# One streaming-encoder layer on one core: 1/rms by a diagonal, another load order, two splits and two bank plans moved

## What is computed

```python
h = rmsnorm(x, g_pre_mix)                   # x * rsqrt(mean(x*x) + eps) * g, a token per row
z = h @ w_in                                # 1024 -> 1440 mixer columns + 2048 gate logits
q = rmsnorm(z[:, 0:384], g_q) @ w_uq        # latent attention: queries
ckv = rmsnorm(z[:, 384:640], g_kv)          # latent keys and values
a = latent_attention(q, ckv, rope(kpe))     # prompt (chunk-causal) and sample against the cache
b = window_attention(rope(qs), rope(ks), vs, sinks)   # chunks of 64 frames, 192 keys, a sink per head
m = sigmoid(gate_a) * (a @ w_branch[0]) + sigmoid(gate_b) * (b @ w_branch[1])
x = x + rmsnorm(m @ w_out, g_post_mix)
x = x + rmsnorm(swiglu(rmsnorm(x, g_pre_ffn)), g_post_ffn)
```

## Time and profile before

| | us |
|---|---|
| median of three runs | 919.78 |
| lowest, highest | 918.79, 921.39 |
| the profiled execution itself | 920.1 |
| its span, first to last instruction | 918.3 |
| TensorE busy in it | 880.5 |
| VectorE busy | 485.5 |
| ScalarE busy | 390.5 |
| GpSimd busy | 75.8 |
| mean granted clock of TensorE | 0.997 |

### The profile page before, as it was taken

How to read it: one execution, slowest core, us unless ns; L and a number is a source line. 1 busy time by engine, 2 the same in 40 slices (tenths; PEclk the granted TensorE clock), 3 DMA queues, 4 the chain that set the end, 5 groups by cost and what they waited for, 6 DMA issues and landing times.

```text
span 918.3 us, 13750 instructions
## 1 busy us (share of the span) xinstructions
PE 880.5 (96%) x5457; PEld 799.9 (87%) x5457; DVE 485.5 (53%) x745; ACT 390.5 (43%) x771; POOL 75.8 (8%) x73
## 2 busy tenths in 40 slices
PE   4999999999999988999999899999999999999997
PEld 3888899989977776998878899999999998888885
DVE  5523522433344555564668877777777774343124
ACT  5311422244454556452565544445545443332112
POOL 0300198050030000000000000000000000000000
PEclk9999999999999999999999999999999999999999
DMA  6523246062240000654623232223333226322202
GB/s 266 162 87 79 73 112 202 8 188 83 76 106 1 1 1 2 184 176 180 217 92 92 69 90 74 78 82 92 93 92 92 76 86 223 98 69 92 70 24 115
DMA packets 101452, 91.92 MB, mean 100 GB/s; under 512 B 8480, under 2 KB 85296, under 8 KB 101248
## 3 DMA queue, kind: packets, MB, share of 16 engines
q1 hardware_dynamic: 95072, 85.93, 30.3%
q10 hardware_dynamic: 5424, 3.25, 1.2%
q0 software_dynamic: 896, 1.92, 0.6%
HBM read 79.60 MB, written 12.40 MB: 100 GB/s over the span
## 4 chain that ended last, share of the span: by engine, by line
PE 91%; ACT 3%; DVE 3%; DMA 1%; issue 1%; DVEq 0%; ACTq 0%
PE ps L1142 27%; PE ps L1144 26%; PE ps L1143 26%; PE ps L1316 2%; PE ps L1365 1%; PE ps L1327 1%; PE ps L1412 1%; PE ps L1286 1%; PE ps L1359 1%; PE ps L1290 1%; DVE nm_c L1687 1%; ACT probs L871 1%; PE ps L1389 1%; PE ps L1399 1%; DMA x_t<-in_x_prompt 1%
## 5 line engine op out<-in xcount | busy, mean ns | idle before, releaser
L1624 DVE TENSOR_TENSOR wlo<-raw,whi 128x1024 fp32r<-128x1024 f32 x59 | 77.4, 1315 | 212.1 <-ACT whi L800 204.6
L800 ACT ACTIVATE whi<-raw 128x1024 fp32r<-128x1024 f32 x59 | 62.0, 1056 | 178.6 <-PE ps L1144 169.6
L1142 PE MATMUL ps<-h_hi,wlo 128*128 128x320 f32 x288 | 90.9, 316 | 1.9 <-DVE z L1664 1.0
L1144 PE MATMUL ps<-h_hi,whi 128*128 128x320 f32 x288 | 89.0, 309 | 0.0
L1143 PE MATMUL ps<-h_lo,whi 128*128 128x320 f32 x288 | 88.9, 309 | 0.0
L1142 PE MATMUL ps<-sc_hi,t_lo 128*128 128x320 f32 x252 | 78.0, 309 | 3.9 <-ACT u L1057 2.9
L1144 PE MATMUL ps<-sc_hi,t_hi 128*128 128x320 f32 x252 | 77.8, 309 | 0.0
L1143 PE MATMUL ps<-sc_lo,t_hi 128*128 128x320 f32 x252 | 77.8, 309 | 0.0
L1047 ACT ACTIVATE t_hi<-wd 128x512 fp32r<-128x512 f32 x84 | 52.8, 629 | 58.6 <-DVE wd L1883 52.8
L1142 PE MATMUL ps<-whi,gu_lo 128*128 128x512 f32 x190 | 74.0, 390 | 0.3 <-DVE gu_lo L1955 0.3
L1143 PE MATMUL ps<-wlo,gu_hi 128*128 128x512 f32 x190 | 73.9, 389 | 0.0
(11 more groups left out here) (302 smaller groups left out, 2135.4 us busy)
## 6 DMA issues: line engine op xcount, KB each, us to landing
raw<-in_w_gate_up SPq DMA_DIRECT2D x44, 512.0 KB, 3.8
raw<-in_w_down SPq DMA_DIRECT2D x22, 512.0 KB, 3.7
raw<-in_w_in SPq DMA_DIRECT2D x16, 512.0 KB, 4.0
raw<-in_w_in SPq DMA_DIRECT2D x12, 480.0 KB, 4.3
gates_scratch<-gate_s SPq DMA_DIRECT2D x16, 320.0 KB, 2.4
gate_r<-gates_scratch SPq DMA_DIRECT2D x8, 640.0 KB, 4.0
raw<-in_w_branch SPq DMA_DIRECT2D x8, 512.0 KB, 4.7
raw<-in_w_out SPq DMA_DIRECT2D x8, 512.0 KB, 5.6
```

Source lines behind the costliest of these rows:

```text
L800: act.activation(whi[:, r % 2, :] if to is None else to, raw[:, r, :], ACT.Copy).then_inc(w_hi, 1)
L1142: pe.matmul(out, left[1], right[0], start=first, stop=False, skip_group_check=not own_group)
L1144: return pe.matmul(out, left[0], right[0], start=False, stop=last, skip_group_check=not own_group)
L1624: dve.tensor_tensor(lo[:, place, :], raw[:, r, :], hi[:, place, :].bitcast(F32), ALU.subtract).then_inc(w_lo, 1)
```

## The change

1. **1/rms apart from the norm weight.** VectorE multiplies x by the norm weight into a new tile `xg` as soon as both have landed (`h_gain`). 1/rms goes on the diagonal of a 128x128 tile `diag_r` (two of them in turn), and `h_turn` multiplies each block of `xg` by it with an ordinary fp32 matmul in place of a transpose.
2. **Loads.** `gpre_b` moves from ScalarE's queue to SyncE's, second in order; slot 0 then comes ahead of tile 1, and slot 1 ahead of tile 2.
3. **Order in the opening.** A `Sqrt` on a constant stands ahead of the first statistics on ScalarE. TensorE does 24 transposes of the identity into bank 7 before the first turn. On TensorE the turn of tile 1 moves between the two slots of tile 0's product; on ScalarE and VectorE the statistics of tile 1 and the split of slot 1 move behind tile 0's parts.
4. **z chunks in rotating banks**: chunk c and tile t in bank (5c + t) mod 8, and gate 0 waits for 10, gate 1 for 12 emptied banks. TensorE's, and VectorE's, loops there are written out.
5. **Late splits.** On ScalarE and VectorE what belongs to the eighth gate slot (the logits' copy and the split of slot 21) moves behind the 15 transposes' jobs.
6. **Sinks.** `job_bank` is turned by one, so the last two jobs lie in banks 6 and 7. VectorE writes the sinks when all but these two are emptied, and does its last job behind them. TensorE waits for the last two jobs only before the first two `chunk_values`, which use banks 6 and 7.

```diff
 def job_bank(j):
-    return 4 + j % 4 if j < JOBS1 else (j - JOBS1) % 4
+    return 4 + (j + 3) % 4 if j < JOBS1 else (j - JOBS1) % 4
...
             load_x(0)
-            load_x(1)
+            sp.dma_start(gpre_b[:], g_pre_mix.to_broadcast([P, D])).then_inc(gpre_in, 16)
             for j in range(2):
                 load(j, win_v[:, 2 * j:2 * j + 2, 0:IN_CHUNK], IN_CHUNK)
-            for t in range(2, TILES):
+                load_x(j + 1)
+            for t in range(3, TILES):
                 load_x(t)
...
         def _(act):
-            act.dma_start(gpre_b[:], g_pre_mix.to_broadcast([P, D])).then_inc(gpre_in, 16)
...
             act.wait_ge(eps_rdy, 1)
+            act.activation(sd_h[:, 7:8], eps_c[:, 0:1], ACT.Sqrt).then_inc(table_rdy, 1)
...
-            for j in range(8):
+            def first_logits(j):
                 if j >= 2:
-
                     act.wait_ge(g_st[j % 2], 16 * (j // 2))
                 logits_out(G0, 0, j, gate_s, 2 * (j % 2))
-            for j in range(JOBS1):
+
+            for j in range(7):
+                first_logits(j)
+            for j in range(3 * TILES):
+                job(j)
+            first_logits(7)
+            for j in range(3 * TILES, JOBS1):
                 job(j)
...
             def h_turn(t):
-                pe.wait_ge(h_norm, t + 1)
+                pe.wait_ge(h_xg, t + 1)
+                pe.wait_ge(h_diag, t + 1)
...
-                        ins = pe.transpose(ps[:, 5 + n % 3, k * P:(k + 1) * P], x_t[:, t, c:c + P], ident[:])
+                        ins = pe.matmul(ps[:, 5 + n % 3, k * P:(k + 1) * P], xg[:, t, c:c + P], diag_r[:, t % 2, :],
+                                        start=True, stop=True)
...
             pe.wait_ge(const_rdy, 1)
+            for n in range(24):
+                pe.transpose(ps[:, 7, 0:P], ident[:], ident[:])
             h_turn(0)
             for t in range(TILES):
-                if t + 1 < TILES:
+                if t and t + 1 < TILES:
                     h_turn(t + 1)
...
+                    if t == 0 and k == 2:
+                        h_turn(1)
...
-            with pe.Fori(0, 2) as it:
+            for chunk in (1, 2):
+                def z_bank_free(t):
+                    if 5 * chunk + t >= 8:
+                        pe.wait_ge(bank_empty, 5 * chunk + t - 7)
+
                 for j in range(4):
-                    tall(it * 4 + (4 + j + 1), j % 2, IN_CHUNK, h_hi, h_lo, 2 * j, KD - 1,
-                         lambda t: pe.wait_ge(bank_empty, it * 5 + (t + 1)), z_mm)
-
+                    tall(4 * chunk + j + 1, j % 2, IN_CHUNK, h_hi, h_lo, 2 * j, KD - 1, z_bank_free, z_mm, 5 * chunk)
+
+            for j in range(8):
+                pe.wait_ge(w_lo, G0 + j + 1)
+                if j < 2:
+                    pe.wait_ge(bank_empty, 10 + 2 * j)
+                b = 2 * (j % 2)
+                wide(j % 2, h_hi, h_lo, (b, b + 1), 0, KD, KD).then_inc(w_used, 1)
             pe.wait_ge(bank_empty, 15)
...
-            job_emptied(pe, JOBS1 - 2)
-            job_emptied(pe, JOBS1 - 1)
...
+                if c < 2:
+                    job_emptied(pe, JOBS1 - 2 + c)
...
+            def h_gain(t):
+                dve.wait_ge(x_in[t], 16)
+                dve.tensor_tensor(xg[:, t, :], x_t[:, t, :], gpre_b[:], ALU.mult).then_inc(h_xg, 1)
+
...
-                dve.scalar_tensor_tensor(out=x_t[:, t, :], in0=x_t[:, t, :], scalar=r_h[:, t:t + 1], in1=gpre_b[:],
-                                         op0=ALU.mult, op1=ALU.mult).then_inc(h_norm, 1)
-
+                if t >= 2:
+                    dve.wait_ge(h_tr, 2 * t - 2)
+                dve.tensor_scalar(diag_r[:, t % 2, :], ident[:], r_h[:, t:t + 1], None, ALU.mult).then_inc(h_diag, 1)
...
-            dve.wait_ge(job_act, JOB_COUNTS[JOBS1 - 1][0])
-            dve.wait_ge(job_dve, JOB_COUNTS[JOBS1 - 1][1])
+            dve.wait_ge(job_act, JOB_COUNTS[JOBS1 - 3][0])
+            dve.wait_ge(job_dve, JOB_COUNTS[JOBS1 - 3][1])
```

More of the change, by code:

```diff
@@ L323, in build_layer @@
     x_t = area("x_t", [P, TILES, D], 10240)
+    xg = area("xg", [P, TILES, D], 20480)
+    diag_r = area("diag_r", [P, 2, P], 32800)
     junk_h = area("junk_h", [P, D], 27680)
@@ L443, in build_layer @@
         eps_rdy, pad_rdy, const_rdy, sink_rdy = sem("eps_rdy"), sem("pad_rdy"), sem("const_rdy"), sem("sink_rdy")
-        h_ssq, h_sd, h_rs, h_norm, h_tr, h_hi_rdy, h_lo_rdy = (sem(n) for n in ("h_ssq", "h_sd", "h_rs", "h_norm", "h_tr", "h_hi_rdy", "h_lo_rdy"))
+        h_ssq, h_sd, h_rs, h_xg, h_diag, h_tr, h_hi_rdy, h_lo_rdy = (sem(n) for n in ("h_ssq", "h_sd", "h_rs", "h_xg", "h_diag", "h_tr", "h_hi_rdy", "h_lo_rdy"))
+        table_rdy = sem("table_rdy")
         bank_empty = sem("bank_empty")
@@ L1636, in h_scale @@
                 dve.wait_ge(h_rs, t + 1)
-                dve.scalar_tensor_tensor(out=x_t[:, t, :], in0=x_t[:, t, :], scalar=r_h[:, t:t + 1], in1=gpre_b[:],
-                                         op0=ALU.mult, op1=ALU.mult).then_inc(h_norm, 1)
+                if t >= 2:
+                    dve.wait_ge(h_tr, 2 * t - 2)
+                dve.tensor_scalar(diag_r[:, t % 2, :], ident[:], r_h[:, t:t + 1], None, ALU.mult).then_inc(h_diag, 1)
+            dve.wait_ge(const_rdy, 1)
             dve.wait_ge(gpre_in, 16)
+            h_gain(0)
             h_scale(0)
             split_lo(1, 0)
-            split_lo(2, 1)
             for t in range(TILES):
-                if t + 1 < TILES:
+                if t and t + 1 < TILES:
+                    h_gain(t + 1)
                     h_scale(t + 1)
@@ L1654, in _, with z_out @@
                                       h_hi[:, to[0], to[1]].bitcast(F32), ALU.subtract).then_inc(h_lo_rdy, 1)
+                if t == 0:
+                    h_gain(1)
+                    h_scale(1)
+                    split_lo(2, 1)
             split_lo(5, 0)
             split_lo(6, 1)
-            def z_out(it, chunk, cols):
+            def z_out(chunk):
                 for t in range(TILES):
                     if t < TILES - 1:
-                        dve.wait_ge(z_mm, it * 4 + (4 * chunk + t + 1))
+                        dve.wait_ge(z_mm, 4 * chunk + t + 1)
                     else:
-                        dve.wait_ge(w_used, it * 4 + 4 * (chunk + 1))
-                    dve.tensor_copy(z[:, t, cols], ps[:, t, 0:IN_CHUNK]).then_inc(bank_empty, 1)
-            z_out(0, 0, slice(0, IN_CHUNK))
-            with dve.Fori(0, 2) as it:
-                for j in range(4):
-                    if j == 3:
-                        z_out(it, 1, bass.ds(it * IN_CHUNK + IN_CHUNK, IN_CHUNK))
-                    after_slot(4, it, j)
+                        dve.wait_ge(w_used, 4 * (chunk + 1))
+                    dve.tensor_copy(z[:, t, chunk * IN_CHUNK:(chunk + 1) * IN_CHUNK],
+                                    ps[:, (5 * chunk + t) % 8, 0:IN_CHUNK]).then_inc(bank_empty, 1)
+            z_out(0)
+            for j in range(8):
+                if j % 4 == 3:
+                    z_out(j // 4 + 1)
+                after_slot(4, 0, j)
             dve.wait_ge(tab_in, 16 * 4)
@@ L1726, in job @@
                 ins.then_inc(job_dve, 1)
-            with dve.Fori(0, 2) as it:
-                for j in range(4):
-                    after_slot(G0, it, j)
-            for j in range(JOBS1):
+            for j in range(7):
+                after_slot(G0, 0, j)
+            for j in range(3 * TILES):
+                job(j)
+            after_slot(G0, 0, 7)
+            for j in range(3 * TILES, JOBS1 - 2):
                 job(j)
@@ L1737, in _ @@
             dve.wait_ge(sink_in, 16)
-            for u in range(2):
-                dve.wait_ge(g_st[u], 16 * 4)
-            dve.wait_ge(job_act, JOB_COUNTS[JOBS1 - 1][0])
-            dve.wait_ge(job_dve, JOB_COUNTS[JOBS1 - 1][1])
+            dve.wait_ge(job_act, JOB_COUNTS[JOBS1 - 3][0])
+            dve.wait_ge(job_dve, JOB_COUNTS[JOBS1 - 3][1])
             for u in range(2):
@@ L1747, in _ @@
                                     sink_b[rows, u:HEADS:2].rearrange("p (g c) -> p g c", g=KV_HEADS)).then_inc(probs_rdy, 1)
+            for j in range(JOBS1 - 2, JOBS1):
+                job(j)
+            for u in range(2):
+                dve.wait_ge(g_st[u], 16 * 4)
             def chunk_max(c):
```

11 lines of the change are left out of this document (4 added, 7 removed).

## The result

The changed kernel takes 912.54 us, the median of 4 runs (911.14 to 914.03), against 920.5 (918.79 to 921.39) for the kernel before on the same chip: a ratio of 0.992, with a 95% interval of 0.9898 to 0.9943. The direction was right and the time lies in the range, 2.0 us above the forecast of 910.5. The profiled execution took 912.8 us (before: 920.1).

The account below looks back on a forecast made before the run. The prediction took TensorE to bound the kernel, so only its waits and half-clock time could be won. From 920.1 us it subtracted 3.8, 1.1, 3.2 and 1.5 to reach 910.5, with a range of 908.8 to 914.0.

Parts of the forecast that it names:

- z chunks: Ahead of gate 0: rotating banks remove TensorE's 1.04 us wait; gain 1.1 us (0.7 to 1.2).
- z transposes: Stage from first z transpose to first `uq` matmul: 10.65 us becomes 7.45 with later splits; gain 3.2 (1.5 to 3.6).
- sinks: Ahead of the window scores: the wait of 1.39 us and a wake-up go; gain 1.5 (1.2 to 1.55).
- rival of late stores: z transposes stay slow through late stores of z or a falling clock: 1.7 us less gain, 912.2; chance 0.12.
- old trace behind 190 us: Everything behind 190 us was expected to run as before, shifted by 9.6 us.
- Opening: Start up to the `in_hi` matmuls: earlier root and scaling let them begin at 30.9, not 34.7; gain 3.8 (2.5 to 4.6).
- Matmul for transpose: Turns of x: 40 fp32 matmuls at 0.118 us against 0.109 a transpose; +0.4 us, hidden behind VectorE.
- VectorE's 4.2: Opening, tiles 3 and 4: VectorE's summed work of 4.2 us each, taken to set the pace.
- TensorE needs less than 4.2 for a tile: Opening: TensorE takes 3.49 us a tile, 0.87 for the turn and 2.62 for 12 matmuls, so VectorE decides.
- forecast of 30.9: End of the opening: TensorE two products behind tile 3's low parts at 25.6, so at 30.9 us.
- half clock in the opening: TensorE at half clock in tiles 0 and 1: at worst 0.5 us, mostly hidden by VectorE's chain.
- slower rival: Opening: fp32 matmuls at four times a transpose make turns the bound; 924.1 us, deciding from about 0.35 a matmul; chance 0.03.

Follow-up runs that it names:

- e9: Changed kernel with z chunks in banks 0 to 4 again, with the former waits for them and the gates: 912.89 us.
- e7: Changed kernel with both waits for the last two projections ahead of the first scores again, their copies ahead of the sinks on VectorE: 915.41 us.
- e8: Changed kernel with the eighth gate slot's split and logits' copy ahead of the z transposes' evictions again: 916.15 us.
- e1: Kernel before, with only the 40 turns of x made ordinary fp32 matmuls by the identity: 922.03 us, one run.
- e6: Changed kernel with x scaled by one instruction, true transposes, 32 warm-up transposes ahead of turn 0 and 18 behind it: 909.35 us.
- e2: Changed kernel with x scaled in place by one VectorE instruction and true transposes, the rest as changed: 909.43 us.
- e3: Changed kernel with 48 instead of 24 transposes of the identity ahead of the first turn: 913.41 us.
- e4: Changed kernel without the 24 transposes of the identity ahead of the first turn: 913.63 us.
- e11: e6 with 8 and 24 transposes of the identity filling TensorE's two gate/up waits near 493 and 498 us: 908.02 us.

## Why the prediction was right, and where it was off

**z chunks (1.1), z transposes (3.2) and sinks (1.5)** came as worked out: 1.1, 3.2 and 1.5 in the trace. e9 and e7 give 1.0 and 1.4 when their parts are undone. For the z transposes the stage was put at 7.45 and took 7.46, with PEclk 1.00, and e8 splits the gain into the two causes that the prediction named (2.0 of wait, where it also said 2.0, and 1.2 for the rest, which it put at 1.7 of clock; e8's trace, without that fall, lacks this 1.2). The rival of late stores did not come up: the `uq` matmul waits for nothing. The old trace behind 190 us is shifted as expected, but for 0.4, which no run explains.

**Opening (3.8): measured 1.2**, below the 2.5 that the prediction gave as this term's own bound. The total stayed in the range only because the other three came to their full size and the range covers 5 us; that is luck as far as the opening goes. The step that failed is "32 in 3.77 us, 0.118 each", under *Matmul for transpose*. The row counts 32 instructions, and the step took them for 32 matmuls of the code. They are 16 in the code, four `qabs` jobs of four, each of which stands in the trace as two instructions; so one costs 0.236 us, twice the 0.109 of a transpose. With that a turn is 1.70 instead of 0.87 (e1), TensorE needs 4.39 a tile, more than VectorE's 4.2, and the sentence "TensorE needs less than 4.2 for a tile" falls as well. The bound of the opening changed engines. The code at L1282 would have given it away: a count of how often that line is reached gives 16, against the 32 of the row.

VectorE's 4.2 was too high as well: it was summed from durations, and the rows of a tile follow each other faster than that. VectorE in the changed kernel, the same instruction for tiles 3 and 4:

```profile
18.59 1.21 DVE L1655 TENSOR_TENSOR xg<-x_t,gpre_b 128x1024 f32<-128x1024 f32 x1
...
22.45 1.21 DVE L1655 TENSOR_TENSOR xg<-x_t,gpre_b 128x1024 f32<-128x1024 f32 x1
```

3.86 us a tile.

At full clock this opening has its first product at 11.73 to 11.84 and `in_hi` at 32.1 to 32.2 (e7, e8 and e9, which share it: 32.11, 32.13, 32.21). That is a gain of 2.5 to 2.6, so the wrong bound took 1.2 to 1.3 of the missing 2.6 us. The turns themselves cost 3.0 (see e6). The forecast of 30.9 lay 1.8 above the 29.1 that true transposes reach at full clock, so only 1.2 of the 3.0 shows as a miss. The other 1.3 to 1.4 are the second term that was off, the **half clock in the opening**. The prediction gave it "at worst 0.5", because VectorE's chain would hide it. With TensorE as the bound nothing hides it. The windows of the changed kernel:

```profile
8.00:9.00 1.00, 0.66 (x3) 0.69 (x4) 0.35 (x2) 0.81 (x1) 0.00 (x0) 0.50 1.01 395
9.00:10.00 1.00, 1.00 (x7) 1.00 (x7) 1.00 (x1) 0.00 (x0) 0.00 (x0) 0.50 1.08 429
10.00:11.00 1.00, 1.00 (x6) 1.00 (x6) 0.07 (x1) 0.58 (x1) 0.00 (x0) 0.50 1.03 422
```

Turn 0 took 3.40 us here, 2.02 in e7. The warm-up did raise the clock, but its 24 transposes ended at 5.8, and TensorE then stood still for 2.57 us.

What the prediction had right about the opening: the first turn at 8.0 (8.34), VectorE's reciprocal and diagonal at 0.45 (0.44), the landings of slot 0 and `gpre_b`. The **slower rival** had the right mechanism, turns that become the bound, with the wrong price: at 0.213 us a matmul (1.70 / 8) it stays below the 0.35 from which it decides. It came true by half.

The Trainium skill ("FP8 and Floating Point Precision", TensorE Precision Notes) gives true fp32 four passes. Measured here are two instructions and twice a transpose's time, which seems half of what the page says. The prediction had set the four against a transpose, and the rows show that to be the wrong measure. The fp32r matmuls of the split products take 0.218 us for 480 columns (2.62 / 12), 0.45 ns a column; an ordinary fp32 matmul takes 0.213 for 128, 1.66 ns a column, 3.7 times as much; a transpose, at 0.109, takes 0.85 and so is no cheap unit itself. Against the fp32r matmul the trace nearly agrees with the page. Its other page ("Perfetto Trace Analysis", Transposes: do logical transposes as transposes) was right, and the price is 2.9 us for 40 of them by e2, 3.0 at full clock. Against the third ("TensorE: Matmul & The Clock Gate", Part 4: transposes don't count as busy for the clock) stands e3: 48 transposes and nothing else ran ahead of a turn at the full pace (1.95), and in e4, with none, it ran at half (3.75).

**Totals against milestones.** The forecast came out 2 us low: 2.6 for the opening less 0.4 gained at the end leaves 2.2 of the profiled 912.8 against 910.5. By the repeated runs (912.05 and 912.54) the same stands. The best version is e11: the changed order with plain scaling and true transposes, TensorE kept busy in the opening and in two later waits; 908.02 us, 10.8 us or 1.1% less than the kernel before on its chip, where the change as made gets 0.8%.

## What to carry to other kernels

A price read from a grouped row is per instruction of the trace; before it enters a sum, count how many instructions one operation of the code leaves there, and do it for both sides of an exchange. When a term is hidden "behind VectorE", write the other engine's sum beside it with the upper price: here 4.2 against 3.49 looked safe, while in truth 3.86 stood against 4.39. And when two versions differ by 1 or 2 us, compare milestones of the traces, the granted clock behind them and each run's mean granted clock, since a fall of the clock elsewhere can hide the difference in the total.
